# A gated linear recurrence stage: its convolution on TensorE, its root and scan one piece behind

## The chip, the cores and the metric

The kernel runs on one core of one Trainium2 chip. The metric is the device time of one execution in microseconds: 8486.05 us is the median of three runs before the change (8471.72 to 8500.62).

## The reference

One inference step of a decoder layer: projection, sparse attention, a recurrent branch, an output projection, a mixture of experts. The change touches the recurrent branch alone. It works on 512 channels for a prompt of 4096 positions and for 8 sequences of 4 new positions with stored states:

```python
def rglru_branch(xr, yg, conv_prev, h_prev, conv_w, conv_b, rg_wa, rg_ba, rg_wx, rg_bx, rg_lambda):
    n, t, _ = xr.shape
    xp = jnp.concatenate([conv_prev.astype(xr.dtype), xr], axis=1)
    xc = sum(conv_w[j] * xp[:, j:j + t] for j in range(CONV_WIDTH)) + conv_b
    conv_new = xp[:, t:]
    xb = xc.reshape(n, t, RG_BLOCKS, RG_BLOCK_W)
    r = jax.nn.sigmoid(jnp.einsum('ntkc,kcd->ntkd', xb, rg_wa).reshape(n, t, D_RNN) + rg_ba)
    i = jax.nn.sigmoid(jnp.einsum('ntkc,kcd->ntkd', xb, rg_wx).reshape(n, t, D_RNN) + rg_bx)
    log_a = -RG_C * r.astype(jnp.float32) * jax.nn.softplus(-rg_lambda.astype(jnp.float32))
    a = jnp.exp(log_a)
    b = jnp.sqrt(-jnp.expm1(2.0 * log_a)) * (i * xc).astype(jnp.float32)
    ...
    y = jnp.swapaxes(hs, 0, 1).astype(xr.dtype) * jax.nn.gelu(yg)
    return y, conv_new, h_last.astype(h_prev.dtype)
```

Between b and y stands the scan h = a*h + b along the positions. The outputs of the branch are y (to a scratch array in memory, read by the next stage), the last three convolution inputs and the last h, for the prompt and for each sampled sequence.

## The kernel before

The program is a row of stages (`build`), each closed by a barrier of all engines; inside a stage each engine runs a list of instructions written by hand, and waits on semaphores. The recurrent stage is `phase_recur`. Channels lie along the 128 partitions, so the 512 channels are four chunks c, and a chunk has three pieces k: positions 0 to 2047, 2048 to 4095, and the 32 sampled positions. The twelve pieces are `segs`; piece n is (n // 3, n % 3).

For each piece VectorE convolves (`convolve`: one product with bias, L1347, three multiply-adds, L1349), one piece ahead; TensorE multiplies the result by two block-diagonal gate matrices into PSUM (L1308, L1309); ScalarE makes two sigmoids (r and i, L1286, L1288), tanh (u), the tanh of the GELU, the exponential (a, L1295) and the square root (b, L1297); VectorE makes i*xc (L1360), a*a and the ratio (L1367, L1368), the GELU's product (L1372), the product with the root (L1374), the scan (L1377, with a copy of its last column, L1378) and the last product y (L1385). The 32 sampled positions are four steps of two small products (L1383, L1384) instead of a scan. GpSimd makes the inner polynomial of the GELU in three passes (L1270 to L1274).

SyncE issues all transfers in one order: the weights, `load(0)`, `load(1)`, then for each chunk the store of every piece's y to `rnnT` when its product is done (`y_done`), the prompt's states after piece k = 1, the sampled states after k = 2 (`rglru_sample` and three `conv_sample` stores, 4 bytes per element), and then a wait for these stores and `load(c + 2)`. A load is a chunk's xr and yg of 4096 positions, the 32 sampled columns, and three small loads of stored convolution states. The y, h and `hlast` buffers exist once, so the scan waits until the stores of the piece before have landed (`wait(e, s["stored"], stored_by(c, k))`):

```python
                    e.wait_ge(s["root"], n + 1)
                    ch.link(e.tensor_tensor(gi, gi, b[:, 0:l], ALU.mult))
                    wait(e, s["stored"], stored_by(c, k))
                    if k < 2:
                        ch.link(e.tensor_tensor_scan(h[:, 0:l], a[:, 0:l], gi, hlast[:, :] if k else 0.0, ALU.mult, ALU.add))
```

Of the kernel before, what the change touches and what calls it, by code (L numbers as in the profile page):

```python
# [20 lines left out]
P = 128  # L21
D = 1024
DC = D // P
SEQ = 4096
# [1159 lines left out]
def phase_recur(nc, A, S):  # L1184

    SEG = 2048
    with ExitStack() as ctx:
# [15 lines left out]
        names = "zeroed params chunk0 chunk1 conv gates r_done i_done a_done u_done ratio root inner tanh mult y_done stored act_own own pool_own consts softplus e1".split()  # L1203
# [3 lines left out]
        stored_by = lambda c, k: 16 * (9 * c + (0, 1, 4)[k])  # L1207
# [5 lines left out]
        with nc.Block() as block:  # L1213
            @block.sync
            def _(e):
# [22 lines left out]
                for c in range(RC):  # L1238
                    q = c % 2
                    at = slice(c * P, (c + 1) * P)  # L1240
                    for k in range(3):
                        e.wait_ge(s["y_done"], 3 * c + k + 1)
                        dst = slice(k * SEG, k * SEG + L(k))
                        e.dma_start(S["rnnT"][c, :, dst], y[:, 0:L(k)]).then_inc(s["stored"], 16)
                        if k == 1:
                            e.dma_start(S["rglru_prompt"][0:1, at].rearrange("o p -> p o"), hlast[:, :]).then_inc(s["stored"], 16)
                            e.dma_start(S["conv_prompt"][:, at].rearrange("j p -> p j"), x[:, q, SEQ:]).then_inc(s["stored"], 16)
                        if k == 2:
                            e.dma_start(S["rglru_sample"][:, at].rearrange("q p -> p q"),
                                        h[:, 0:SR].rearrange("p (q t) -> p q t", t=DECQ)[:, :, DECQ - 1]).then_inc(s["stored"], 16)  # L1250
                            for j in range(3):
                                e.dma_start(S["conv_sample"].rearrange("(q j) c -> q j c", j=3)[:, j, at].rearrange("q p -> p q"),
                                            xw[:, q, :, DECQ + j]).then_inc(s["stored"], 16)
# [3 lines left out]
                e.wait_ge(s["stored"], stored_by(RC, 0))  # L1257

            @block.gpsimd
            def _(e):  # L1260
# [3 lines left out]
                for n, (c, k) in enumerate(segs):  # L1264
                    src = yg[:, c % 2, k * SEG:(k + 1) * SEG] if k < 2 else ys[:, c % 2, :]
                    gg = gg2[:, n % 2, 0:L(k)]
                    loaded(e, c)
                    wait(e, s["y_done"], n - 1)
                    wait(e, s["pool_own"], 2 * n)
                    e.tensor_tensor(gg, src, src, ALU.mult).then_inc(s["pool_own"], 1)  # L1270
                    e.wait_ge(s["pool_own"], 2 * n + 1)
                    e.tensor_scalar(gg, gg, 0.044715, 1.0, ALU.mult, ALU.add).then_inc(s["pool_own"], 1)
                    e.wait_ge(s["pool_own"], 2 * n + 2)
                    e.tensor_tensor(gg, gg, src, ALU.mult).then_inc(s["inner"], 1)  # L1274

            @block.scalar
            def _(e):
                e.wait_ge(s["consts"], 1)
                e.activation(sp[:, 1, :], sp[:, 0, :], ACT.Exp, scale=-1.0).then_inc(s["e1"], 1)
                e.wait_ge(s["softplus"], 1)  # L1280
                for n, (c, k) in enumerate(segs):
                    l = L(k)
                    gi, gg = gi2[:, n % 2, 0:l], gg2[:, n % 2, 0:l]
                    e.wait_ge(s["gates"], n + 1)
                    wait(e, s["a_done"], n)
                    e.activation(r[:, 0:l], pa[:, 0:l], ACT.Sigmoid, bias=vec[:, 1, c:c + 1]).then_inc(s["r_done"], 1)  # L1286
                    wait(e, s["y_done"], n - 1)
                    e.activation(gi, px[:, 0:l], ACT.Sigmoid, bias=vec[:, 2, c:c + 1]).then_inc(s["i_done"], 1)  # L1288
# [1146 lines left out]
```

## Time and profile before

| what | value |
|---|---|
| median of three runs | 8486.05 us |
| the profiled execution: its own time | 8488.34 us |
| its span (first to last instruction) | 8486.2 us |
| busy in the span: TensorE, VectorE, ScalarE, GpSimd | 74%, 52%, 46%, 13% |
| the recurrent stage in it | from 5525 to 6032 us of the span |
| mean granted TensorE clock, share of full speed | 0.873 |

The busy shares are means over stages with different limits; the recurrent stage is some 6% of the span. Times in rows are microseconds from the start of the span. In the names, `rc_` tiles belong to the recurrent stage; PE is TensorE, DVE VectorE, ACT ScalarE, POOL GpSimd, SP SyncE; PEld is TensorE's load of weights. An f32 matmul leaves two MATMUL rows.

### The profile page before, as it was taken

What the parts mean: (1) busy time and instruction counts of PE and PEld (TensorE: products, weight loads), DVE (VectorE), ACT (ScalarE), POOL (GpSimd) and SP (SyncE); (2) the same over time, 40 slices, a digit from 0 to 9 for tenths busy, and PEclk for the clock granted to TensorE, in tenths of its full rate; (3) what the DMA queues carried; (4) which work ended last, traced back from release to release, by engine and by line L of the source; (5) the groups of instructions that cost most, each with busy time, mean ns of one, the idle gap of its engine ahead of it and who ended that gap; (6) DMA issues with size and microseconds to landing.
All of it is one profiled execution on the core that took longest, in us unless ns stands there. A gap on an engine that the chain in (4) does not pass through costs nothing. (4 is left out here: it accounts for less than half of the span.)

```text
span 8486.2 us, 113111 instructions
## 1 busy us (share of the span) xinstructions
PE 6263.9 (74%) x38431; PEld 4189.0 (49%) x38714; DVE 4448.6 (52%) x10781; ACT 3943.1 (46%) x7822; POOL 1095.8 (13%) x1571
## 2 busy tenths in 40 slices
PE   6999975887887788788888761711499929999950
PEld 2777752555555455555555541600255527667740
DVE  1122137888777878888888648256255511101126
ACT  0221225788877788888788730133233302212224
POOL 1222210000000000000000000022011143333334
PEclk8999987999999999999999975755688869999985
DMA  5221210000000000000000010234423238888877
GB/s 189 63 59 57 61 53 8 5 9 13 9 11 10 11 11 11 11 11 11 10 11 6 7 64 2 118 67 50 85 89 99 84 104 336 323 321 333 333 271 253
DMA packets 329210, 759.17 MB, mean 89 GB/s; under 512 B 123534, under 2 KB 187022, under 8 KB 285769
## 3 DMA queue, kind: packets, MB, share of 16 engines
q0 software_dynamic: 71520, 432.08, 13.8%
q1 hardware_dynamic: 257236, 321.70, 13.3%
q8 instruction: 222, 3.64, 0.2%
q14 instruction: 178, 1.45, 0.1%
q10 hardware_dynamic: 54, 0.30, 0.0%
HBM read 589.37 MB, written 162.62 MB: 89 GB/s over the span
## 5 line engine op out<-in xcount | busy, mean ns | idle before, releaser
L953 PE MATMUL at_pC<-at_mark,at_identb 128*128 128x256 bf16 (+1 forms) x5708 | 758.0, 283 | 382.8 <-DVE at_mark L1088 302.5
L1010 DVE CUSTOM_DVE_ANT_0 at_sm<-at_pS,at_drop 128x512 f32<-128x512 f32 (+3 forms) x1152 | 696.3, 642 | 319.3 <-PE at_pS L909 317.0
L953 PEld LDWEIGHTS at_pC<-at_mark,at_identb 128*128 128x128 bf16 x5708 | 531.9, 101 | 637.8 <-DVE at_mark L1088 462.6
L844 ACT ACTIVATE at_sm<-at_sm,at_negm 128x512 f32<-128x512 f32 (+3 forms) x1152 | 786.0, 696 | 58.8 <-DVE at_negm L1015 58.4
L909 PE MATMUL at_pS<-keep_KT,at_q 64*128 64x512 f32 (+3 forms) x2304 | 649.4, 642 | 205.0 <-DVE at_mx L1010 204.8
L1002 DVE SCALAR_TENSOR_TENSOR at_score<-at_relu,keep_IW,at_score 128x512 f32<-128x512 f32 (+3 forms) x994 | 660.5, 707 | 120.0 <-ACT at_relu L829 116.4
L930 PEld LDWEIGHTS at_pO<-at_pt_sb,keep_V 128*64 128x64 f32 x8448 | 471.7, 142 | 416.8 <-issue 290.5
L899 PE MATMUL at_pD<-keep_IKT,at_iq_stack 128*128 128x512 bf16 (+3 forms) x1989 | 521.1, 375 | 167.1 <-ACT at_relu L829 95.3
L829 ACT ACTIVATE at_relu<-at_pD 128x512 f32<-128x512 f32 (+3 forms) x1136 | 583.5, 569 | 104.6 <-PE at_pD L899 62.2
L919 PE MATMUL at_pT<-keep_ident,at_sm 128*128 128x128 f32 x4224 | 587.6, 281 | 40.9 <-DVE at_out L1024 32.5
L930 PE MATMUL at_pO<-at_pt_sb,keep_V 128*64 128x128 f32 x8448 | 614.5, 288 | 0.1
L2225 DVE TENSOR_TENSOR ex_gu<-ex_pg,ex_sg 128x256 f32<-128x256 f32 x98 | 41.6, 425 | 988.0 <-ACT ex_sg L2207 988.0
L919 PEld LDWEIGHTS at_pT<-keep_ident,at_sm 128*128 128x128 f32 x4224 | 474.0, 143 | 106.6 <-issue 96.2
L479 PE MATMUL pj_ptm<-keep_w_in,pj_hT 128*128 128x512 f32 (+1 forms) x1584 | 516.2, 488 | 0.0
L410 DVE TENSOR_TENSOR pj_ra<-pj_z,pj_rope 128x256 f32<-128x256 f32 x66 | 42.9, 651 | 858.0 <-ACT pj_z L384 858.0
L1791 POOL MEMSET sa_IQB<- 128x1024 f32 x1 | 1.0, 952 | 3773.3 <-POOLq L68 3773.3
L865 ACT ACTIVATE at_mark<-at_key_low,at_sigma 128x1536 bf16<-128x1536 uint16 (+15 forms) x390 | 451.6, 1165 | 73.8 <-DVEq L1084 73.1
L494 PE MATMUL pj_pcm<-pj_hT,keep_w_in 128*128 128x128 f32 x4224 | 477.1, 275 | 0.0
L494 PEld LDWEIGHTS pj_pcm<-pj_hT,keep_w_in 128*128 128x128 f32 x4224 | 474.3, 192 | 0.0
L835 ACT ACTIVATE at_pt_sb<-at_pT 128x512 f32<-128x512 f32 (+3 forms) x576 | 321.7, 559 | 302.5 <-PE at_pT L919 301.3
L2172 PE MATMUL ex_pg<-ex_wg,ex_xT 128*128 128x256 f32 x1568 | 379.5, 397 | 88.7 <-DMA ex_wu<-in_exp_w_up,ex_wi 83.0
L865 ACT ACTIVATE at_mark<-at_key_high,at_sigma 128x1280 bf16<-128x1280 int16 (+15 forms) x364 | 421.3, 1163 | 47.2 <-DVEq L1084 46.3
(418 smaller groups left out, 10910.2 us busy)
## 6 DMA issues: line engine op xcount, KB each, us to landing
scratch_ys<-ex_y SPq DMA_DIRECT2D x98, 512.0 KB, 2.7
ada_w_sb<-in_ada_w SPq DMA_DIRECT2D x12, 2048.0 KB, 8.1
scratch_x<-mx_x SPq DMA_DIRECT2D x33, 512.0 KB, 6.5
scratch_h<-mx_h SPq DMA_DIRECT2D x33, 512.0 KB, 2.7
cb_x<-scratch_x SPq DMA_DIRECT2D x33, 512.0 KB, 4.2
pj_x<-in_x_prompt SPq DMA_DIRECT2D x32, 512.0 KB, 3.5
mx_x<-in_x_prompt SPq DMA_DIRECT2D x32, 512.0 KB
out_y_prompt<-cb_out SPq DMA_DIRECT2D x32, 512.0 KB, 2.9
```

Source lines behind the costliest of these rows:

```text
L479: last = e.matmul(ptm[:, n, 0:b - a], hT[:, par, k, :], w[:, k, a:b], start=k == 0, stop=k == DC - 1)
L494: last = e.matmul(pcm[:, c // RC, c % RC, :], w[:, k, C_XR + c * P:C_XR + (c + 1) * P], hT[:, par, k, :], start=k == 0, stop=k == DC - 1)
L829: e.activation(r[:, n % 4, 0:b - a], pD[:, n % 2, 0:b - a], ACT.Relu).then_inc(s["relu"], 1)
L844: last = e.activation(row, row, ACT.Exp, bias=negm[:, x.group % 16, kv:kv + 1], scale=-1.0, accum_out=den[:, x.side, kv * G + x.g, x.c:x.c ...
L865: last = e.activation(mark[:, at], (lo if low else hi)[:, at], ACT.Sign, bias=trial, scale=-2.0 ** (v.what - (STRICT if low else HIGH)), a ...
L899: last = e.matmul(pD[:, n % 2, 0:b - a], IQH[:, side, k, h, :], keys[:, k, a:b], start=k == 0, stop=k == 1)
L909: last = e.matmul(pS[:, kv, 0:x.width], Q[rows, x.side, x.g, :], KT[rows, x.a:x.a + x.width], start=True, stop=True)
L919: last = e.transpose(pT[:, kv, j:j + P], sm[:, u % RING, kv, j:j + P], ident)
L930: last = e.matmul(pO[rows, x.g, :], V[:, (x.a + j) // P, rows], PTs[:, u % 2, kv, j:j + P], start=x.first and x.g == 0 and j == 0, stop=x. ...
L953: last = e.matmul(pC[:, side, 0:b - a], identb[:, :], mark[:, a:b], start=a == at.start, stop=not constant and b == at.stop)
L1002: e.scalar_tensor_tensor(at, r[:, n % 4, 0:b - a], w, at, ALU.mult, ALU.add).then_inc(s["acc"], 1)
L1010: last = e.tensor_tensor_reduce(sm[:, u % RING, kv, 0:x.width], pS[:, kv, 0:x.width], drop[:, o:o + x.width], -HD ** -0.5, -NEG, ALU.add, ...
```

## The change

The convolution moves from VectorE to TensorE: VectorE builds, once, sixteen 128 x 128 matrices with a tap's weights on the diagonal (`taps`), TensorE adds up four products per 512 columns in PSUM (`shift`), and ScalarE copies the sum out with its bias (`unload`). TensorE and the sigmoids now work in halves of 1024 columns, m = 0 to 19 (`halves`). ScalarE takes the GELU as one function, so GpSimd keeps only a small copy per chunk. The root of a piece stands behind the next piece's exponential (`root(n - 1)`), and on VectorE the product with the root, the scan and the last product stand behind the next piece's ratio (`recurrence(n - 1)`). y is written into the GELU's buffer, two deep; `hlast` and the sampled h have buffers per chunk; the stores have semaphores of their own (`written0/1`, `state0/1`), and no scan waits for them. The diff, cut to its core:

```diff
-    SEG = 2048
+    SEG, HALF = 2048, 1024
...
-        r = sb("rc_r", [P, SEG]); a = sb("rc_a", [P, SEG])
-        u = sb("rc_u", [P, SEG]); t1 = sb("rc_t1", [P, SEG]); t2 = sb("rc_t2", [P, SEG]); b = sb("rc_b", [P, SEG]); h = sb("rc_h", [P, SEG]); y = sb("rc_y", [P, SEG])
-        hlast = sb("rc_hlast", [P, 1])
-        pa = pb("rc_pa", [P, SEG]); px = pb("rc_px", [P, SEG])
+        a2 = sb("rc_a", [P, 2, SEG]); t2 = sb("rc_t", [P, 2, SEG])
+        r = sb("rc_r", [P, SEG]); u = sb("rc_u", [P, SEG]); b = sb("rc_b", [P, SEG]); h = sb("rc_h", [P, SEG])
+        taps = sb("rc_taps", [P, RC, 4, P])
+        hlast = sb("rc_hlast", [P, RC, 2]); hsm = sb("rc_h_sample", [P, RC, SR])
+        pc = pb("rc_pc", [P, 2, HALF]); pa = pb("rc_pa", [P, HALF]); px = pb("rc_px", [P, HALF])
...
+        halves = [(n, at) for n, (c, k) in enumerate(segs) for at in range(0, L(k), HALF)]
+        halves_by = lambda n: sum(m < n for m, _ in halves)
...
-                        e.dma_start(S["rnnT"][c, :, dst], y[:, 0:L(k)]).then_inc(s["stored"], 16)
+                        e.dma_start(S["rnnT"][c, :, dst], gg2[:, (3 * c + k) % 2, 0:L(k)]).then_inc(s[f"written{(3 * c + k) % 2}"], 16)
...
                     if c + 2 < RC:
-                        e.wait_ge(s["stored"], stored_by(c + 1, 0))
+                        e.wait_ge(s[f"state{q}"], 96 * (c // 2 + 1))
                         load(c + 2)
...
+                def unload(m):
+                    n, at = halves[m]
+                    c, k = segs[n]
+                    l = min(HALF, L(k) - at)
+                    e.wait_ge(s["shifted"], m + 1)
+                    wait(e, s["mult"], n - 1)
+                    e.activation(xc2[:, n % 2, at:at + l], pc[:, m % 2, 0:l], ACT.Identity, bias=vec[:, 0, c:c + 1]).then_inc(s["conv"], 1)
+
+                def sigmoids(m):
...
+                    e.wait_ge(s["gates"], m + 1)
+                    wait(e, s["a_done"], n)
+                    e.activation(r[:, at:at + l], pa[:, 0:l], ACT.Sigmoid, bias=vec[:, 1, c:c + 1]).then_inc(s["r_done"], 1)
+                    wait(e, s["y_done"], n - 1)
+                    e.activation(gi2[:, n % 2, at:at + l], px[:, 0:l], ACT.Sigmoid, bias=vec[:, 2, c:c + 1]).then_inc(s["i_done"], 1)
+
+                def root(n):
+                    l = L(segs[n][1])
+                    wait(e, s["y_done"], n)
+                    e.wait_ge(s["ratio"], n + 1)
+                    e.activation(b[:, 0:l], t2[:, n % 2, 0:l], ACT.Sqrt).then_inc(s["root"], 1)
+
+                unload(0)
                 for n, (c, k) in enumerate(segs):
...
+                    for m in range(halves_by(n), halves_by(n + 1)):
+                        if m + 1 < len(halves):
+                            unload(m + 1)
+                        sigmoids(m)
...
+                    wait(e, s[f"written{n % 2}"], 16 * (n // 2))
+                    e.activation(gg2[:, n % 2, 0:l], gate, ACT.Gelu_apprx_tanh).then_inc(s["gelu"], 1)
+                    e.activation(a2[:, n % 2, 0:l], r[:, 0:l], ACT.Exp, scale=c8[:, 1, c:c + 1]).then_inc(s["a_done"], 1)
+                    if n:
+                        root(n - 1)
+                root(len(segs) - 1)
...
+                def shift(m):
+                    n, at = halves[m]
+                    c, k = segs[n]
+                    q = c % 2
+                    loaded(e, c)
+                    if k == 2:
+                        e.wait_ge(s["window"], c + 1)
+                    wait(e, s["conv"], m - 1)
...
+                def gates(m):
+                    n, at = halves[m]
+                    c, k = segs[n]
+                    e.wait_ge(s["conv"], m + 1)
+                    wait(e, s["i_done"], m)
+                    wait(e, s["r_done"], m)
...
+                shift(0)
+                for m in range(len(halves)):
+                    if m + 1 < len(halves):
+                        shift(m + 1)
+                    gates(m)
...
+                for n in range(len(segs)):
+                    ratio(n)
+                    if n:
+                        recurrence(n - 1)
+                recurrence(len(segs) - 1)
```

Three places of the order in which instructions stand. The first is ScalarE in the first chunk, from the sigmoids of the second piece to the root; before:

```order
L1286 ACT_TABLE_LOAD
L1286 ACTIVATE rc_r<-rc_pa,rc_vec 128x2048
L1288 ACTIVATE rc_i<-rc_px,rc_vec 128x2048
L1291 ACTIVATE rc_u<-rc_r,rc_c 128x2048
L1293 ACTIVATE rc_g<-rc_g 128x2048
L1295 ACT_TABLE_LOAD
L1295 ACTIVATE rc_a<-rc_r,rc_c 128x2048
L1297 ACT_TABLE_LOAD
L1297 ACTIVATE rc_b<-rc_t 128x2048
```

And after the change, where L1284 is the copy of a half's convolution and L1300 the root of the piece before:

```order
L1284 ACTIVATE rc_xc<-rc_pc,rc_vec 128x32
L1292 ACTIVATE rc_r<-rc_pa,rc_vec 128x1024
L1294 ACTIVATE rc_i<-rc_px,rc_vec 128x1024
L1311 ACTIVATE rc_u<-rc_r,rc_c 128x2048
L1314 ACT_TABLE_LOAD
L1314 ACTIVATE rc_g<-rc_yg 128x2048
L1315 ACT_TABLE_LOAD
L1315 ACTIVATE rc_a<-rc_r,rc_c 128x2048
L1300 ACT_TABLE_LOAD
L1300 ACTIVATE rc_b<-rc_t 128x2048
L1284 ACTIVATE rc_xc<-rc_pc,rc_vec 128x1024
```

A load of the GELU's table has come in between tanh and the exponential, the root now reads the ratio of the piece before, and the next copy stands behind it. In the whole stage there are 47 table loads where there were 36.

The second place is TensorE at the change from chunk 1 to chunk 2 after the change; L1334 are the tap products, L1346 and L1347 the gates:

```order
L1346 MATMUL rc_pa<-rc_xc,rc_wa 128x512
L1347 MATMUL rc_px<-rc_xc,rc_wx 128x512
L1334 MATMUL rc_pc<-rc_x,rc_taps 128x512 x8
L1346 MATMUL rc_pa<-rc_xc,rc_wa 128x32
L1347 MATMUL rc_px<-rc_xc,rc_wx 128x32
L1334 MATMUL rc_pc<-rc_x,rc_taps 128x512 x8
```

The eight tap products of the new chunk's first half, which read the loaded x, stand ahead of the gates of the old chunk's small piece (128x32). Before, the same place held gates alone:

```order
L1308 MATMUL rc_pa<-rc_xc,rc_wa 128x512
L1309 MATMUL rc_px<-rc_xc,rc_wx 128x512
L1308 MATMUL rc_pa<-rc_xc,rc_wa 128x32
L1309 MATMUL rc_px<-rc_xc,rc_wx 128x32
L1308 MATMUL rc_pa<-rc_xc,rc_wa 128x512
L1309 MATMUL rc_px<-rc_xc,rc_wx 128x512
```

The third place is VectorE after the change, from the second piece's ratio to the first piece's last product:

```order
L1391 TENSOR_TENSOR rc_i<-rc_i,rc_xc 128x2048
L1395 TENSOR_TENSOR rc_t<-rc_a 128x2048
L1396 SCALAR_TENSOR_TENSOR rc_t<-rc_t,rc_u 128x2048
L1404 TENSOR_TENSOR rc_i<-rc_i,rc_b 128x2048
L1407 SCALAR_TENSOR_TENSOR rc_h<-rc_a,rc_i 128x2048
L1408 COPY rc_hlast<-rc_h 128x1
L1416 TENSOR_TENSOR rc_g<-rc_h,rc_g 128x2048
```

The first three rows belong to the second piece, the last four to the first (L1407 is its scan); the four passes of the convolution and the GELU's product are gone from this list.

## Rows read from the trace of the kernel before

**Rows 1.** The page's first line.

```profile
span 8486.2 us, 113111 instructions
```

**Rows 2.** Stretches: length, busy time (instructions) of PE, PEld, DVE, ACT, POOL, granted clock, DMA share, GB/s.

```profile
5561.47:5665.43 103.96, 23.20 (x40) 10.13 (x41) 86.32 (x47) 37.03 (x28) 44.36 (x13) 0.58 0.16 59
5665.43:5766.66 101.23, 20.37 (x39) 8.72 (x38) 65.60 (x43) 35.74 (x27) 25.46 (x9) 0.59 0.47 63
5766.66:5868.90 102.24, 18.09 (x35) 8.01 (x34) 65.87 (x38) 35.74 (x27) 25.53 (x9) 0.58 0.49 62
5868.90:5971.67 102.77, 17.78 (x34) 7.43 (x32) 49.46 (x45) 34.45 (x26) 12.77 (x6) 0.58 0.37 21
5971.67:6032.06 60.39, 0.00 (x0) 0.00 (x0) 0.00 (x1) 0.00 (x0) 0.00 (x0) 0.50 0.60 1
```

**Rows 3.** Waits in the stage: who for whom, total us, times, longest.

```profile
DVE rc_h L1377 <- DMA out_conv_sample<-rc_xw: 72.8, 3, 25.5
...
DVE rc_h L1383 <- DMA out_conv_prompt<-rc_x: 18.2, 4, 16.2
```

**Rows 4.** VectorE's groups in the stage: shapes, count, busy us, mean ns, idle before.

```profile
L1349 DVE SCALAR_TENSOR_TENSOR rc_xc<-rc_x,rc_cw,rc_xc 128x2048 f32<-128x2048 f32 x24 | 85.4, 3556 | 0.9
...
L1347 DVE TENSOR_SCALAR rc_xc<-rc_x,rc_cw,rc_vec 128x2048 f32<-128x2048 f32 x8 | 20.6, 2571 | 8.2 <-DMA rc_xw<-in_state_conv 8.0
...
L1384 DVE TENSOR_TENSOR rc_h<-rc_h,rc_i 128x8 f32<-128x8 f32 x16 | 2.8, 175 | 0.5
```

**Rows 5.** ScalarE in order of time: start, us, instruction, then idle time before.

```profile
5625.19 1.28 ACT L1295 ACT_TABLE_LOAD   x1
5626.48 2.00 ACT L1295 ACTIVATE rc_a<-rc_r,rc_c 128x2048 f32<-128x2048 f32 x1
...
5636.39 0.29 ACT L1286 ACTIVATE rc_r<-rc_pa,rc_vec 128x32 f32<-128x32 f32 x1
```

**Rows 6.** The same view in the stage before: a function over 1056 columns.

```profile
5471.27 1.08 ACT L1825 ACTIVATE sa_lgt<-sa_lgt 128x1056 f32<-128x1056 f32 x1 [7.68 <-DVE sa_lgt L1968]
```

**Rows 7.** VectorE in order of time: a large piece's recurrence.

```profile
5635.37 2.29 DVE L1374 TENSOR_TENSOR rc_i<-rc_i,rc_b 128x2048 f32<-128x2048 f32 x1
5637.70 4.49 DVE L1377 TENSOR_TENSOR_SCAN rc_h<-rc_a,rc_hlast,rc_i 128x2048 f32<-128x2048 f32 x1
...
5642.40 2.29 DVE L1385 SCALAR_TENSOR_TENSOR rc_y<-rc_h,rc_t 128x2048 f32<-128x2048 f32 x1
```

**Rows 8.** TensorE in order of time: one burst of gate products, two rows (x2) each.

```profile
5582.35 2.05 PE L1308 MATMUL rc_pa<-rc_xc,rc_wa 128*128 128x512 f32 x2 [67.36 <-DVE rc_xc L1349]
5584.19 1.92 PE L1309 MATMUL rc_px<-rc_xc,rc_wx 128*128 128x512 f32 x2
5585.89 1.91 PE L1308 MATMUL rc_pa<-rc_xc,rc_wa 128*128 128x512 f32 x2
...
5588.88 1.02 PE L1308 MATMUL rc_pa<-rc_xc,rc_wa 128*128 128x512 f32 x2
5589.74 1.02 PE L1309 MATMUL rc_px<-rc_xc,rc_wx 128*128 128x512 f32 x2
```

**Rows 9.** SyncE's queue: its waits for stores ahead of a load: total us, times, longest.

```profile
SPq L1230 <- DMA out_conv_sample<-rc_xw: 103.2, 2, 52.7
```

**Rows 10.** In order of time: the first load's issue, VectorE's first use, chunk 2's load.

```profile
5543.93 0.58 SPq L1230 DMA_DIRECT2D rc_x<-scratch_xrT  x1
...
5561.47 4.73 DVE L1347 TENSOR_SCALAR rc_xc<-rc_x,rc_cw,rc_vec 128x2048 f32<-128x2048 f32 x1 [7.97 <-DMA rc_xw<-in_state_conv]
...
5718.39 0.35 SPq L1230 DMA_DIRECT2D rc_x<-scratch_xrT  x1
```

**Rows 11.** Tile view of out_conv_sample: its twelve stores, issue to landing.

```profile
DMA to landing us min/median/max: 32.1/44.1/54.4
```

**Rows 12.** Issues in the stage: count, KB each, median us from issue to landing.

```profile
scratch_rnnT<-rc_y SPq DMA_DIRECT2D x8, 1024.0 KB, 5.7
...
out_rglru_sample<-rc_h SPq DMA_DIRECT2D x4, 4.0 KB, 19.9
```

More of the change, by code:

```diff
@@ L1263, in _ @@
                 e.memset(x[:, :, 0:3], 0.0).then_inc(s["zeroed"], 1)
-                for n, (c, k) in enumerate(segs):
-                    src = yg[:, c % 2, k * SEG:(k + 1) * SEG] if k < 2 else ys[:, c % 2, :]
-                    gg = gg2[:, n % 2, 0:L(k)]
+                for c in range(RC):
                     loaded(e, c)
[L1268 to L1274, printed above, removed]
+                    e.tensor_copy(xw[:, c % 2, :, 3:], xs[:, c % 2, :].rearrange("p (q t) -> p q t", t=DECQ)).then_inc(s["window"], 1)
             @block.scalar
@@ L1296, in _ @@
-                    e.wait_ge(s["ratio"], n + 1)
-                    e.activation(b[:, 0:l], t1[:, 0:l], ACT.Sqrt).then_inc(s["root"], 1)
+                    gate = yg[:, c % 2, k * SEG:(k + 1) * SEG] if k < 2 else ys[:, c % 2, :]
+                    wait(e, s[f"written{n % 2}"], 16 * (n // 2))
+                    e.activation(gg2[:, n % 2, 0:l], gate, ACT.Gelu_apprx_tanh).then_inc(s["gelu"], 1)
+                    e.activation(a2[:, n % 2, 0:l], r[:, 0:l], ACT.Exp, scale=c8[:, 1, c:c + 1]).then_inc(s["a_done"], 1)
@@ new lines, in gates @@
+                def gates(m):
+                    n, at = halves[m]
+                    c, k = segs[n]
+                    e.wait_ge(s["conv"], m + 1)
+                    wait(e, s["i_done"], m)
+                    wait(e, s["r_done"], m)
+                    for a in range(0, min(HALF, L(k) - at), CUT):
+                        l = min(CUT, L(k) - at - a)
+                        xc = xc2[:, n % 2, at + a:at + a + l]
+                        e.matmul(pa[:, a:a + l], wa[:, c, :], xc, start=True, stop=True)
+                        last = e.matmul(px[:, a:a + l], wx[:, c, :], xc, start=True, stop=True)
+                    last.then_inc(s["gates"], 1)
@@ L1315, in _ @@
                 e.wait_ge(s["params"], 16 * 28)
+                for c in range(RC):
+                    for j in range(4):
+                        last = e.tensor_scalar(taps[:, c, j, :], S["ident"][:, :], cw[:, c, j:j + 1], None, ALU.mult)
+                last.then_inc(s["taps"], 1)
                 ch.link(e.tensor_scalar(sp[:, 2, :], vec[:, 3, :], -1.0, None, ALU.mult))
@@ L1364, in _ @@
+                    e.wait_ge(s["i_done"], halves_by(n + 1))
+                    e.wait_ge(s["conv"], halves_by(n + 1))
+                    e.tensor_tensor(gi2[:, n % 2, 0:l], gi2[:, n % 2, 0:l], xc2[:, n % 2, 0:l], ALU.mult).then_inc(s["mult"], 1)
                     e.wait_ge(s["a_done"], n + 1)
                     e.wait_ge(s["u_done"], n + 1)
-                    wait(e, s["root"], n)
-                    ch.link(e.tensor_tensor(t1[:, 0:l], a[:, 0:l], a[:, 0:l], ALU.mult))
-                    e.scalar_tensor_tensor(t1[:, 0:l], t1[:, 0:l], 1.0, u[:, 0:l], ALU.add, ALU.mult).then_inc(s["ratio"], 1)
@@ L1370, in _, with recurrence @@
-                    src = yg[:, c % 2, k * SEG:(k + 1) * SEG] if k < 2 else ys[:, c % 2, :]
-                    e.wait_ge(s["tanh"], n + 1)
-                    ch.link(e.scalar_tensor_tensor(t2[:, 0:l], gg2[:, n % 2, 0:l], 1.0, src, ALU.add, ALU.mult))
+                    wait(e, s["root"], n - 1)
+                    ch.link(e.tensor_tensor(t, a, a, ALU.mult))
+                    e.scalar_tensor_tensor(t, t, 1.0, u[:, 0:l], ALU.add, ALU.mult).then_inc(s["ratio"], 1)
+                def recurrence(n):
+                    c, k = segs[n]
+                    l = L(k)
+                    a, gi, gg = a2[:, n % 2, 0:l], gi2[:, n % 2, 0:l], gg2[:, n % 2, 0:l]
+                    e.wait_ge(s["mult"], n + 1)
```

88 lines of the change are left out of this document (28 added, 60 removed).

## The prediction

> **What bounds the kernel now.** The page's first line gives the span, 8486.2 us [rows 1]; the profiled execution took 8488.34 us, 2.3 us over the median of the runs. The change touches one stage alone, so I read the view of stretches, cut where the first load lands and where the last product of each chunk ends [rows 2]. The four chunks take 104.0, 101.2, 102.2 and 102.8 us, and after the last product 60.4 us pass in which nothing computes until the next stage starts. In a chunk VectorE is busy for 49 to 86 us, ScalarE for some 36, TensorE for some 20: VectorE sets the pace, with gaps. The view of waits says what the gaps are [rows 3]: three times, 72.8 us together, a scan waits until the 4-byte stores of the chunk before have landed, and 18.2 us more go to the small store of the prompt's convolution state. The groups show the largest single piece of VectorE's work: the convolution costs 85.4 + 20.6 = 106.0 us in the eight large pieces [rows 4].
>
> I number the pieces 0 to 11 (pieces 2, 5, 8 and 11 are the small ones, of 32 columns) and write y0 to y11 for the end of a piece's last product. Before, y2, y5, y8 and y11 are 5665.4, 5766.7, 5868.9 and 5971.7 [rows 2]. All that follows y11 is the same 60.4 us, so the whole forecast is one number: where y11 comes to stand.
>
> **The change, part by part.** *Prices.* A ScalarE function over 2048 columns takes 2.0 us, a table load 1.28, so that the function starts 1.3 later, and a function over 32 columns 0.3 [rows 5]. For 1024 columns I take 1.1, by a row of 1056 columns [rows 6]. On VectorE the product with the root, the scan (4.49), its copy and the last product take 2.3 + 4.5 + 0.2 + 2.3 = 9.3 us for a large piece [rows 7]; for a small one eight steps of 0.175 and two small products, some 2.1 with their links [rows 4]. An f32 matmul of 512 columns is two rows: in a burst's first 6 us one starts 1.70 us after the other (the engine at 1.2 GHz), later 0.86 (2.4 GHz) [rows 8]. Eight tap matmuls, one half piece, are thus 6.9 to 13.6 us, four gate matmuls 3.4 to 6.8. I take the fast end plus 2.6 for the first 6 us after a long idle, since the burst shown became fast after some 6 us, and 4.7 for gates behind a short idle; the ends go into the range.
>
> *Engine sums.* VectorE loses the convolution and the GELU's product, and keeps five passes of 2.3 and a scan, 16.2 us per large piece. TensorE has 24 matmuls where there were 8: 20.6 us. ScalarE has six half functions, four whole ones and four table loads, 6.6 + 8.0 + 5.2 = 19.8 us. GpSimd's three GELU passes go. If these ran side by side a piece would cost 20.6 us against more than 25 before; they do not.
>
> *A loop through three engines.* ScalarE's second sigmoid of piece n waits for y(n-2), whose buffer it reuses. The root of piece n-1 now stands behind the exponential of piece n, and y(n-1) needs that root. So from one product to the next everything is in a row: sigmoid 1.1, the second half's gates 4.7, two sigmoids 2.1, tanh 2.0, load 1.3, GELU 1.9, load 1.3, exponential 2.0, load 1.3, root 1.9, VectorE 9.3: 28.9. VectorE's ratio of piece n ends 1.5 us after that root and stands ahead of the recurrence, and handovers cost some 0.7: about 31 us for a large piece.
>
> *First chunk.* The load lands at 5561.5 as before [rows 10]. The 16 products that make the tap matrices fit the 7.97 us in which VectorE waits there [rows 10]; if they took longer, each us would be added once. TensorE does three shifts and two gate groups, 32 matmuls, 27.5 + 2.6: 5591.6. Sigmoids to exponential of piece 0, 10.6: 5602. Copy, load and sigmoids of piece 1's first half 4.5, gates 5.3, sigmoids 2.1, tanh to exponential 8.5, load and root 3.2, VectorE's ratio 1.5, then 9.3: y0 is 5637. Piece 2's GELU waits until the store of piece 0 has landed, 5.7 [rows 12]; its rest and the root of piece 1 take 5.0, VectorE 9.3: y1 is 5657. Then 1.1 + 4.7 + 2.1 + 8.5, the ratio of piece 3 (4.6), the small recurrence 2.1 and handovers: y2 is 5681, 15.6 us later than now.
>
> *Chunk changes.* SyncE's order stays: store y2, the 4-byte stores, wait for them, load the next chunk. From y2 to the load's issue 53.0 us pass [rows 2, 10], 51.6 of it the wait itself in the mean of the two [rows 9], and the load lands 17.5 us after its issue [rows 10]. Now VectorE has no scan that waits for these stores; instead the wait moves to the load. TensorE's shift of the next chunk's first half stands ahead of the small piece's gates, and ScalarE's copy ahead of its sigmoids (both shown by the order above). So pieces 5 and 4 cannot end before the load: 53.0 + 17.5 + shift 9.5 + copy, small functions, four loads and root 4 9.6 + VectorE 9.3 + handovers 1.1 = 100: y4 is 5781. What covers this is piece 3 and the sums of piece 4 alone, some 31 us after y2; ScalarE then stands idle for about 60 us where VectorE stood for some 24. Another 23 as for y2, with the gates faster: y5 is 5804, and a chunk takes 123 us against 101.2. The second change is the same: y8 is 5927.
>
> *The last chunk.* No load follows, so no such wait. But SyncE sends the store of piece 9 (y9 is 5927 + 31 = 5958) behind four 4-byte stores issued at y8. Three of these land 32.1, 44.1 and 54.4 us after their issue, each some 11 behind the one before, where one ahead of them takes 19.9 [rows 11, 12]: landings come in the order of issue. I therefore let store 9 land with them, at 5981, not 5.7 us after its issue. GELU 11 waits for it, and root 10 stands behind GELU 11: 5.0 + 9.3, then the small piece's root and recurrence and handovers 3.7: y11 is 5999.
>
> The sum: 5999 - 5971.7 = 27.3 us later. 8488.3 + 27.3 - 2.3 = **8513 us**. A measurement here tells 0.3% (25.5 us) from no change, so this lies just past that line.
>
> *Where pages of the Trainium skill speak to this.* On the table loads, "ScalarE: Activation LUTs", section "What ACT_TABLE_LOAD costs", puts every switch of set at 2.66 us, drain included, and tells authors to batch by set; the change makes 47 loads of 36. In this trace a function starts 1.3 us after its load began, so the trace decides and the page's price is not used. By it the 11 added loads would cost 29 us where 1.3 gives 14, and the time would be some 15 us longer. On the order of landings, "DMA: Bandwidth & Descriptors", section "Queues, rings and completion order", says a transfer's semaphore write lands only after every earlier write of that DMA engine. That is what I let store 9 do; no row of before has a large store behind 4-byte ones.
>
> **The rivals.**
> *Large stores overtake the small ones.* Store 9 then lands at 5964, GELU 11 is no longer held by it, and y11 is about 5981, 9 us later: 8496 us. Against it stand the landings in order [rows 11]; for it, that no row shows a large store in this place.
> *Faster: the 4-byte stores land sooner.* Both chunk changes and the 60.4 us at the end hang on that landing, so each us of it counts three times. It decides from 9 us on: at 44 instead of 53 the stage is as long as now. If all landed like the first one, in 19.9 [rows 12], 3 x 33 us would go: 8414 us. For it: the stores now read small buffers of their own. Against it: number, size and target of the stores are unchanged, and both waits of before agree [rows 9].
> *TensorE stays at 1.2 GHz.* Its gaps in the loop (up to 11 us while VectorE scans) may keep it slow, as the granted clock of 0.58 to 0.59 in the chunks shows for now [rows 2]. Then a large piece is 24 x 1.70 = 41 us, first of all on TensorE: some 10 us more than the loop for each of eight pieces and a few for each shift behind a load, about 85 to 110 in all: 8600 to 8625 us. Against it: 16 to 24 matmuls per piece in long runs, and the burst of before became fast after some 6 us [rows 8].
>
> **How the numbers follow.** Forecast 0.62, overtaking 0.17, sooner landings 0.07, slow clock 0.06, the rest (a cover or a wait I misjudged, to either side) 0.08. The forecast's own range is 8500 to 8530: gates and shifts at the fast end take 7 us off, at the slow end they add 2.1 per loop. The range for 8 in 10 takes in overtaking and, above, slow gates in most loops: 8490 to 8540. Slower by over 0.3% is somewhat more than half of the forecast (27 against a line of 25.5, and its upper side is wider) plus the slow clock: 0.53. Within 0.3%: the rest of the forecast, and overtaking: 0.38. Faster: 0.09.
>
> **What would show it.** Right: in the changed profile TensorE's first shift of a new chunk ends an idle time of some 60 us, released by the load, twice; the stretches y2 to y5 and y5 to y8 are about 123 us; the convolution is gone from VectorE, which is busy for some 37 us of a chunk; ScalarE waits for a store's landing ahead of the last GELU, and a large piece that nothing holds takes about 31 us from product to product. Wrong: chunks under 105 us, a load that is issued less than 44 us after its chunk's last product, a product-to-product time near 21 us, or a granted clock of half speed through the stage.

## The result, and the profile after

| | before | changed |
|---|---|---|
| median of 5 runs | 8483.35 us (8470.90 to 8500.62) | 8445.29 us (8420.11 to 8446.83) |
| ratio, 95% interval | | 0.9948 (0.9935 to 0.9961) |
| profiled execution | 8488.34 us | 8446.37 us |
| stage: issue of its first load to the next stage's first load | 488.1 us | 424.0 us |

The changed kernel is 0.5% faster; the forecast was 0.3% slower. The stage is 64 us shorter, but all that follows it took 2477.7 us in this execution against 2454.1. That remainder spread from 2449 to 2480 us over the runs below and differed by 12 us between two executions of one and the same kernel, so from here on I compare lengths of the stage, each from one profile. They too spread: the kernel before with both placing edits below took 411.4 us in one execution and 393.4 in another, so differences well under 18 us tell little.

The page's first line [rows 1]:

```profile
span 8444.6 us, 113983 instructions
```

The view of stretches, cut as before at the small pieces' last products, y2, y5, y8 and y11 (the first begins near the landing of the first load) [rows 2]:

```profile
5561.00:5677.67 116.67, 88.65 (x203) 39.37 (x202) 41.18 (x30) 65.80 (x55) 0.21 (x1) 0.89 0.13 48
5677.67:5777.47 99.80, 49.85 (x108) 21.99 (x108) 34.30 (x27) 45.28 (x39) 0.22 (x1) 0.74 0.38 64
5777.47:5876.10 98.63, 46.74 (x108) 20.86 (x108) 34.31 (x27) 45.27 (x39) 0.21 (x1) 0.76 0.42 65
5876.10:5928.10 52.00, 6.08 (x12) 2.66 (x12) 27.49 (x24) 23.58 (x22) 0.00 (x0) 0.57 0.47 33
5928.10:5966.90 38.80, 0.00 (x0) 0.00 (x0) 0.03 (x1) 0.00 (x0) 0.00 (x0) 0.50 0.36 11
```

VectorE's busy time (third column) fell from 66 to 34 us a chunk, and the two middle chunks are hardly shorter: no engine is busy for more than half of them. What is much shorter is the last chunk, 52.0 us in place of 102.8, and the stretch at the end, where nothing computes: 38.8 us in place of 60.4.

The waits in the stage:

```profile
PE rc_pc L1334 <- DMA rc_xw<-in_state_conv: 127.7, 3, 45.8
...
ACT rc_xc L1284 <- PE rc_pc L1334: 102.9, 5, 37.2
...
ACT rc_g L1314 <- DMA scratch_rnnT<-rc_g: 4.7, 2, 2.6
...
SPq L1232 <- DMA out_conv_sample<-rc_xw: 58.3, 2, 29.8
```

No scan waits for a store any more [rows 3]. TensorE waits for the load, ScalarE for TensorE, and SyncE for the stores ahead of the load, as forecast; but SyncE's two waits are 58.3 us together, not 103.2 [rows 9]. The cause is the landing of the state stores, that is the time from a store's issue until its semaphore tells that it is done. The tile view of out_conv_sample gives the shortest, the median and the longest, against 32.1/44.1/54.4 [rows 11]; the issues give the median of the large stores and of rglru_sample, against 5.7 and 19.9 [rows 12]:

```profile
DMA to landing us min/median/max: 15.6/22.7/31.7
```

```profile
scratch_rnnT<-rc_g SPq DMA_DIRECT2D x8, 1024.0 KB, 5.9
...
out_rglru_sample<-rc_h_sample SPq DMA_DIRECT2D x4, 4.0 KB, 14.4
```

The 4-byte state stores land in half to three quarters of the time. The large stores take as long as before, and number and size of the packets are the same. SyncE's issues in order of time show it once: store of y2, the state stores, then the load of chunk 2, now 31.2 us behind the store of y2 [rows 10]:

```profile
5677.67 0.33 SPq L1246 DMA_DIRECT2D scratch_rnnT<-rc_g  x1
5678.05 0.43 SPq L1251 DMA_DIRECT2D out_rglru_sample<-rc_h_sample  x1
5678.52 1.83 SPq L1254 DMA_DIRECT2D out_conv_sample<-rc_xw  x3
5708.90 0.35 SPq L1232 DMA_DIRECT2D rc_x<-scratch_xrT  x1
```

### The profile page after: what moved, and what is told of

It is laid out like the page before. It is cut to its first block and busy times, and to the rows that moved or that the text cites. A ratio compares the mean times of both kernels' runs of the same rounds, so it can differ in the third digit from the quotient of the medians.

```text
span 8444.6 us, 113983 instructions
## 1 busy us (share of the span) xinstructions
PE 6401.7 (76%) x39002; PEld 4242.0 (50%) x39002; DVE 4319.9 (51%) x10733; ACT 3981.5 (47%) x7869; POOL 994.8 (12%) x1539
## 5 line engine op out<-in xcount | busy, mean ns | idle before, releaser
L844 ACT ACTIVATE at_sm<-at_sm,at_negm 128x512 f32<-128x512 f32 (+3 forms) x1152 | 786.3, 697 | 58.7 <-DVE at_negm L1015 58.3
L899 PE MATMUL at_pD<-keep_IKT,at_iq_stack 128*128 128x512 bf16 (+3 forms) x2272 | 585.2, 378 | 141.9 <-ACT at_relu L829 89.6
L919 PE MATMUL at_pT<-keep_ident,at_sm 128*128 128x128 f32 x4224 | 588.6, 282 | 40.9 <-DVE at_out L1024 32.5
```

The source lines that it names most:

```text
L844: last = e.activation(row, row, ACT.Exp, bias=negm[:, x.group % 16, kv:kv + 1], scale=-1.0, accum_out=den[:, x.side, kv * G + x.g, x.c:x.c ...
L899: last = e.matmul(pD[:, n % 2, 0:b - a], IQH[:, side, k, h, :], keys[:, k, a:b], start=k == 0, stop=k == 1)
L919: last = e.transpose(pT[:, kv, j:j + P], sm[:, u % RING, kv, j:j + P], ident)
```

## The experiments

Six theories are told apart. **A, S, W:** the small source tile, the separate counts, or GpSimd's silence (or the GELU function) make the 4-byte stores land sooner. **G:** where the program or its outputs lie in memory does. **L:** the order one piece behind costs time. **T:** the landing can be taken off the path by issuing those stores earlier. "Landings" are those of rglru_sample (median), and of the three conv_sample stores as min/median/max. The runs were made on several chips, on which the kernel before took 8478 to 8503 us in the median; each ratio is against the kernel before on the same chip. The diffs are cut to their core (`...`).

**The two kernels once more**, unchanged.

> The kernel before, unchanged, profiled a second time. In the first profile the 4-byte stores at a chunk's end land 19.9 us (rglru_sample) and 32.1/44.1/54.4 us (three conv_sample stores) after their issue; in the changed kernel 14.4 and 15.6/22.7/31.7. Theory A (the change's own buffers, above all the small tile that the sampled state is stored from, make the stores land sooner): here again about 20 and 32 to 54, and from the last product to the next stage about 60 us. Theory B (how fast such stores land belongs to the run or to where the outputs lie in memory, not to an edit): here some other value, such as 14 and 16 to 32, with the last product to the next stage near 39 us; each us of it counts about twice to three times in the time.

> The changed kernel, unchanged, profiled a second time. Theory A: again about 14 and 16 to 32 us from issue to landing, 30 us from a chunk's last product to the next load's issue, 39 us at the end. Theory B: another value than in its first profile, and the same as in the other kernels of this chip.

Before: 8482.27 us, landings 20.3 and 30.8/42.8/53.6, stage 482.7. Changed: 8442.12 us, 14.8 and 16.6/24.9/33.3, stage 428.1. The landing belongs to the kernel, not to the run.

**A small source tile alone.**

```diff
+hsm = sb("rc_h_sample", [P, RC, SR])
...
-    h[:, 0:SR].rearrange(...)[:, :, DECQ - 1]).then_inc(s["stored"], 16)
+    hsm[:, c, :].rearrange(...)[:, :, DECQ - 1]).then_inc(s["stored"], 16)
```

> The kernel before with one part of the change: the sampled steps write h into a small tile of their own (128 x 4 x 32), which rglru_sample is stored from; all else as before. Theory A: rglru_sample lands in about 14 us instead of 20 and the conv_sample stores in 16 to 32, so the stage ends some 40 to 60 us sooner. Theory B: the same landings as the unchanged kernel on this chip, and the same time within 10 us.

8500.24 us, landings 19.1 and 29.9/42.8/54.2: as before. A falls, and with it the reason that the prediction gave for its rival of sooner landings.

**Own buffers and separate counts alone**, in the kernel before.

```diff
-dma_start(S["rnnT"][c, :, dst], y[:, 0:L(k)]).then_inc(s["stored"], 16)
+dma_start(S["rnnT"][c, :, dst], y[:, n % 2, 0:L(k)]).then_inc(s[f"written{n % 2}"], 16)
...
-e.wait_ge(s["stored"], stored_by(c + 1, 0))
+e.wait_ge(s[f"state{q}"], 96 * (c // 2 + 1))
...
-wait(e, s["stored"], stored_by(c, k))
```

> The kernel before with one part of the change alone: the stored states in buffers of their own, two y buffers and the four counts in place of the one, so that the scan no longer waits for the stores of the chunk before (convolution on VectorE, tanh GELU and the order of the functions stay). Theory S (the one shared count, or the waits on it, makes the landing of the 4-byte stores long): landings fall to about 14 us for rglru_sample and 16, 24, 32 us for conv_sample, the load of chunk 2 is issued 31 us behind the small piece's product, and the time is 8350 to 8385. Theory G (landing is a property of the program as a whole, its memory or its code's place, and not of these waits): landings stay at 20 and 32, 43, 54 us, the wait of 73 us leaves VectorE's scan and the load is issued 53 us behind the product as before; chunks 1 and 3 are then bound by VectorE's own some 68 us (two large pieces of some 27 us and a small one), chunk 2 by its load, and the time is 8380 to 8430. If the wait only moves (rival M, as the prediction had it), chunks stay near 100 us and the time is within 20 us of the kernel before.

8417.95 us, ratio 0.9910 (0.9890 to 0.9931). Tile view of out_conv_sample:

```profile
DMA to landing us min/median/max: 32.2/42.9/55.1
```

S falls: the landing is as long as before, and the load is issued 53.5 us behind the store of y2 (5658.2 to 5711.7). The time falls all the same, to chunks of 89, 88 and 63 us, since the pieces of the other chunk now run during that wait. In this order of the functions the wait moved to the load and was mostly covered.

**A longer program**: 160 memsets of one column on GpSimd, where it waits for the load.

```diff
+for i in range(160):
+    e.memset(junk[:, i:i + 1], 0.0)
```

> The kernel before with 160 memsets of one column each on GpSimd at the start of the recurrent stage, while GpSimd would wait for the load: they change the length of the program and nothing that the stage waits for. Theory G (the place of code or buffers in memory sets the landing of the 4-byte stores): the landings may move from 20 and 32, 43, 54 us by several us, in either direction. Theory S (waits and counts set it): landings within 2 us of those of the kernel before, time within 20 us of it.

8488.96 us, landings 20.0 and 31.0/42.7/54.1: unmoved. Only the prompt's two small stores moved, conv_prompt's from 18.0 us to 10.7.

**GELU as one function alone.**

```diff
-e.tensor_tensor(gg, src, src, ALU.mult)
...
-e.activation(gg, gg, ACT.Tanh, scale=math.sqrt(2 / math.pi)).then_inc(s["tanh"], 1)
+e.activation(gg, gate, ACT.Gelu_apprx_tanh).then_inc(s["tanh"], 1)
...
-ch.link(e.scalar_tensor_tensor(t2, gg2, 1.0, src, ALU.add, ALU.mult))
```

> The kernel before with one part of the change alone: GELU as one function of ScalarE, so that GpSimd computes nothing in the stage and VectorE's product of tanh and gate falls away. Theory W (what GpSimd does in the stage, or the table of the GELU function in the program, sets how fast the 4-byte stores land): landings near 14 us for rglru_sample and 16 to 33 us for conv_sample, time 8400 to 8430. Theory G (where the program or its buffers lie in memory) and theory C (the convolution on TensorE): landings stay at 20 and 32, 43, 54 us; VectorE gives back 2.3 us per large piece at most outside the wait, and the time is within 20 us of the kernel before.

8407.95 us, stage 387.2. Tile view of out_conv_sample:

```profile
DMA to landing us min/median/max: 16.8/24.3/31.2
```

This part alone brings the short landing, as W had it; the convolution on TensorE (theory C of the expectation) is not needed for it.

**The outputs elsewhere**: no instruction changes, only the order in which the outputs are declared, or 4 MB of scratch ahead of the other scratch, or both.

```diff
-for name, shape, _ in _OUT:
+for name, shape, _ in reversed(_OUT):
...
-_SCRATCH = [("mod", ...
+_SCRATCH = [("pad", [1024, 1024], F32), ("mod", ...
```

> The kernel before with its outputs declared in the opposite order and one more scratch tensor of 4 MB declared ahead of the others; nothing else. Theory G (the place in memory of the stores' destination sets their landing): landings move from 20 and 32, 43, 54 us by over 5 us, and the time with them, about three us for each us. Theories W and C: landings within 2 us of those of the kernel before.

> The kernel before with outputs declared in the opposite order and 4 MB more scratch, as before_placed, now with an interval. Theory G (the place in memory of the destination sets the landing): landings again near 14.5 us for rglru_sample and 16, 26, 34 for conv_sample, 8395 to 8425, below the changed kernel's 8442. Rival (the single run of before_placed was a chance): 8470 to 8510 with landings of 32, 43, 54.

> The kernel before with its outputs declared in the opposite order alone. Theory G by the order of the outputs: landing near 16, 26, 34 us and 8395 to 8425. If the scratch does it: landings of 32, 43, 54 us and 8470 to 8510.

> The kernel before with 4 MB of scratch declared ahead of the others alone. Theory G by the scratch, which moves what is placed behind it: landings near 16, 26, 34 us and 8395 to 8425. If the order of the outputs does it: landings of 32, 43, 54 us and 8470 to 8510.

Both edits: 8409.18 us in the single run; again, 8392.05 us, ratio 0.9912 (0.9891 to 0.9933). Scratch alone: 8469.42, stage 466.0, landings 18.3 and 28.3/39.0/48.7, about a tenth shorter than before and far from the short ones. The order of the outputs alone: 8394.82, stage 391.2; its tile view of out_conv_sample:

```profile
DMA to landing us min/median/max: 15.9/22.8/30.3
```

So the short landing needs neither the GELU nor any other instruction: it comes with the order of the outputs in the kernel before as it is, and takes 71 to 97 us off its stage. Stretches of the repeated run, cut where the small pieces' y stores are issued, against [rows 2]:

```profile
5557.00:5660.17 103.17, 22.80 (x40) 9.87 (x41) 85.93 (x47) 37.02 (x28) 43.96 (x12) 0.58 0.16 58
5660.17:5741.93 81.76, 20.49 (x38) 8.87 (x37) 65.59 (x43) 35.74 (x27) 25.52 (x9) 0.58 0.42 78
5741.93:5821.10 79.17, 20.61 (x38) 8.87 (x37) 65.69 (x43) 35.74 (x27) 25.52 (x9) 0.59 0.46 81
5821.10:5898.90 77.80, 17.37 (x34) 7.41 (x32) 48.55 (x39) 34.46 (x26) 12.75 (x6) 0.61 0.31 28
5898.90:5933.42 34.52, 0.00 (x0) 0.00 (x0) 0.00 (x0) 0.00 (x0) 0.00 (x0) 0.50 0.52 1
```

VectorE and ScalarE are as busy as in [rows 2], to within an us; the three later chunks are 19 to 25 us shorter each and the end 26. VectorE's waits for conv_sample's landing, in the same run:

```profile
DVE rc_h L1377 <- DMA out_conv_sample<-rc_xw: 4.2, 2, 3.5
```

It was 72.8 [rows 3].

**The changed kernel with its outputs elsewhere**: both edits, and rglru_sample and conv_sample declared first.

```diff
-for name, shape, _ in _OUT:
+for name, shape, _ in _OUT[-2:] + _OUT[:-2]:
```

> The changed kernel with the same two edits. Theory G: landings move from 14 and 16, 24, 33 us by over 5 us. Theories W and C: landings within 2 us of those of the changed kernel, time within 20 us of it.

> The changed kernel with rglru_sample's and conv_sample's outputs declared ahead of the other outputs; nothing else. Theory G: it may fall into either placement. If the landings are 32, 43, 54 us, the load is issued 53 us behind the small piece's product and the time is near my forecast, 8495 to 8530; if they are 16, 24, 33 us, the time stays within 15 us of the changed kernel's 8445 and the try decides nothing.

8441.21 us, landings 15.8 and 16.8/25.2/37.1; 8443.91 us, 16.1 and 16.1/25.2/37.7. Both stay near the short landing, so the changed kernel with the long one was not seen.

**Root and recurrence at once** in the changed kernel.

```diff
-if n:
-    root(n - 1)
+root(n)
...
-    if n:
-        recurrence(n - 1)
+    recurrence(n)
```

> The changed kernel with one part undone: the root stands right behind its own piece's exponential and the recurrence right behind its own ratio, not one piece behind. Theory L (the loop: sigmoid of piece n, gates, sigmoids, tanh, GELU, exponential, root of n-1, recurrence of n-1, sigmoid of n+1, 31 us a large piece, is what a large piece costs): undone, the sigmoid waits for a product two pieces back, a large piece costs ScalarE's 19.8 us plus some 3 to 5 of waiting for the ratio, about 24 to 28 us, and the first product comes at 5617 instead of 5634; the whole is 50 to 75 us faster than the changed kernel, 8370 to 8395 us. The rival (a piece behind is needed to keep ScalarE from waiting for VectorE's ratio, as the change is meant): ScalarE waits 4.6 us for each ratio, and the stage is 20 to 40 us slower than the changed kernel.

8371.77 us, ratio 0.9847 (0.9831 to 0.9864). Its first three chunks, cut in the same way:

```profile
5562.00:5648.48 86.48, 68.68 (x159) 30.79 (x158) 34.40 (x27) 48.47 (x42) 0.21 (x1) 0.89 0.16 58
5648.48:5716.04 67.56, 42.80 (x98) 18.97 (x97) 34.41 (x27) 45.04 (x40) 0.80 (x1) 0.80 0.49 95
5716.04:5790.97 74.93, 46.54 (x108) 20.84 (x107) 34.48 (x27) 45.16 (x40) 0.21 (x1) 0.80 0.46 85
```

L holds: the same instructions take 30 us less in the first chunk, 32 and 24 in the next two. The order one piece behind costs some 70 us of time.

**State stores earlier**: conv_prompt's and conv_sample's stores at the chunk's start, in the changed kernel and in the variant with the root at once; in that variant also behind the first y store of the chunk (only the place differs).

```diff
+e.wait_ge(s["window"], c + 1)
+e.dma_start(S["conv_prompt"]...).then_inc(s[f"early{q}"], 16)
+for j in range(3):
+    e.dma_start(S["conv_sample"]..., xw[:, q, :, DECQ + j]).then_inc(s[f"early{q}"], 16)
...
-e.wait_ge(s[f"state{q}"], 96 * (c // 2 + 1))
+e.wait_ge(s[f"early{q}"], 64 * (c // 2 + 1))
```

> The changed kernel with the conv_prompt and conv_sample stores issued at the start of each chunk, behind the window copy, where their data are already there, and with the load of chunk c+2 waiting for these alone. Theory T (the landing of these stores is on the path at both chunk changes and at the end of the stage): the load of chunk 2 is issued within 3 us of the small piece's product in place of 31, ScalarE's idle times of 36 and 37 us at the chunk changes shrink to 10 to 15, the tail of 39 us falls to 20, and the time falls by 50 to 75 us to 8370 to 8395. Rival (the many small packets take the engines from the large stores, or the loop of the pieces takes the place of the wait): less than 20 us gained.

> The variant with root and recurrence of the same piece at once, and the early stores as well. Theory T and L together: 8310 to 8345, some 30 to 60 us under the variant with root at once alone (8372). Rival (with a shorter loop VectorE is the bound, and the wait at chunk changes was already hidden by it): within 15 us of 8372.

> Root and recurrence of the same piece at once, and the conv_prompt and conv_sample stores issued right behind the y store of the chunk's first piece in place of the chunk's start. Theory Q (in the variant with the stores at the chunk's start the gain was given back because the y store of the first piece, which a GELU waits for, and the issues of the load queue behind the 4-byte packets): ScalarE's waits for y stores of 25 us in all go to under 5, chunk changes stay free of the landing, and the time is 8310 to 8340. Rival (the packets of load and stores take the same engines wherever they are issued): 8350 to 8370, as with the stores at the chunk's start.

In the changed kernel nothing is gained: 8445.87 us, ratio 0.9942 (0.9922 to 0.9963), stage 434.2. The load is issued within 1 us of the store of y2 and the end is 20 us, as T had it, but T's 50 to 75 us did not come: the y store now queues behind the 4-byte stores, and a GELU waits for it. ScalarE's wait and the tile view of rc_g:

```profile
ACT rc_g L1316 <- DMA scratch_rnnT<-rc_g: 62.3, 4, 28.0
```

```profile
DMA to landing us min/median/max: 1.4/8.4/41.7
```

With the root at once: 8360.11 us, ratio 0.9856 (0.9829 to 0.9884), stage 350.8; behind the first y store 8370.15 us, 0.9854 (0.9836 to 0.9873), stage 349.4, where 360.3 and a ratio of 0.9847 were. No gain is shown: the ratios are no lower, and 10 us of stage are less than two executions of one kernel differed by. ScalarE still waits for y stores, 25.4 us in the one place and 16.6 in the other, where under 5 were expected of the second.

**Own buffers and one GELU**, convolution on VectorE, order as before, outputs and scratch placed as in the run with both edits; then also the stores of conv_prompt and conv_sample behind the first y store, conv_sample's out of rc_xs.

> The kernel before with two parts of the change, own buffers for the stored states and GELU as one function, its convolution still on VectorE and its order as it was, and the outputs and scratch placed as in before_placed. Theory (at the fast landing the tap matrices and the order one piece behind are what costs): chunks of 62 to 70 us bound by VectorE, the next stage starts near 5880, and the time is 8320 to 8375, below both kernels. Rival (the load's 31 us wait and its 17.5 us landing are not covered by the other chunk's pieces): chunks near 80 us, 8380 to 8410.

> As own_buffers_gelu_placed, with the conv_prompt and conv_sample stores issued behind the y store of the chunk's first piece (conv_sample's from rc_xs, which holds the same numbers) and the load of chunk c+2 waiting for these alone. Theory (the tail behind the last product, 41 us there, is their landing; chunk changes are already covered): the tail falls to 20 to 25 us, chunks stay at 70 us, and the time is 8325 to 8340, 15 to 25 us under that variant. Rival (as with the early stores before: y stores and loads queue behind the small packets and give it back): within 10 us of it.

8352.22 us, ratio 0.9855 (0.9839 to 0.9872), stage 348.5; with early stores 8355.42, 0.9838 (0.9821 to 0.9855), stage 346.4. Stretches of the first:

```profile
5637.43:5708.50 71.07, 20.18 (x37) 8.64 (x36) 52.36 (x40) 39.91 (x30) 0.00 (x0) 0.62 0.54 90
5708.50:5780.03 71.53, 20.65 (x37) 8.89 (x36) 52.36 (x40) 39.92 (x30) 0.00 (x0) 0.60 0.54 89
5780.03:5844.20 64.17, 18.07 (x34) 7.71 (x32) 44.04 (x36) 38.63 (x29) 0.00 (x0) 0.61 0.43 34
5844.20:5885.96 41.76, 0.00 (x0) 0.00 (x0) 0.00 (x0) 0.00 (x0) 0.00 (x0) 0.50 0.55 1
```

Without tap matrices this is level with the root at once and beats both kernels. Early stores again brought no gain, where 15 to 25 us were expected: the end is 39.7 us, since rglru_sample's store then lands 23.7 to 34.3 us after its issue, behind the others.

## Why the prediction was wrong

**The step that failed** is the landing of the state stores: "From y2 to the load's issue 53.0 us pass" and "All that follows y11 is the same 60.4 us". Both were carried over from before. Measured: 31.2 and 32.5 us, and 38.8. The prediction had this as a rival, at a chance of 0.07, "each us of it counts three times": 3 x 22 = 66 us off 8513 gives 8447, and 8446.37 was measured. Its reasons did not decide it: small buffers of their own did not shorten the landing, and the same number, size and target of the stores did not keep it. (That it fits so closely has luck in it: the last chunk counted the landing a fourth time, and the 23.6 us more behind the stage took that back.) Two of the prediction's own signs of being wrong came true, chunks under 105 us (99.8 and 98.6) and a load issued less than 44 us after its chunk's last product; both follow from a landing that is 22 us shorter.

| us | forecast | measured |
|---|---|---|
| y0, y1, y2 | 5637, 5657, 5681 | 5634.2, 5653.2, 5677.6 |
| y2 to y4, y2 to y5 | 100, 123 | 76.1, 99.8 |
| y8 to y9 (a large piece that nothing holds) | 31 | 31.1 |
| y8 to y11 | 72 | 52.0 |
| y11 to the next stage | 60.4 | 38.8 |

**What was right.** The loop through three engines is 31.1 us, and its undoing gave 70 us. The first chunk is late by 12 us where 16 were forecast. The wait moved from VectorE's scan to the load; ScalarE's idle time there is 37 us, short of the forecast 60 by little more than the landing. That the loss would have shown at the old landing is an estimate: both the kernel before (stage 391 to 411 us with the short landing, three runs; 483 and 488 with the long one) and the forecast (515 with the long one, 424 to 436 measured with the short one, four runs) differ by nearly the same, some 80 to 90 us, as four terms of some 21 do.

**The change itself, at equal landing, is a loss of the size forecast**: mean stages 429 against 399 us, and ratios of 0.9948 (0.9935 to 0.9961) against 0.9912 (0.9891 to 0.9933), 0.36% or some 31 us, and single runs on one chip, both kernels with both placing edits, 8441.21 against 8409.18; the forecast was 27. It lies where the forecast put it. Stretch by stretch, against the repeated run of the kernel before at the short landing, the first chunk is 13.5 us longer (forecast 15.6), the next two 18.0 and 19.5 (22 and 21), the last 25.8 shorter (31), and the end 4.3 longer (0). What made the changed kernel faster than the kernel before is the landing, and of the change's parts the one-function GELU is the one with which it came.

**Table loads.** The GELU's load starts at 5688.67 and its function at 5689.96:

```profile
5688.67 1.28 ACT L1314 ACT_TABLE_LOAD   x1
5689.96 1.91 ACT L1314 ACTIVATE rc_g<-rc_yg 128x2048 f32<-128x2048 f32 x1
```

It is 1.29 us, as for the other sets; the 2.66 us of the Trainium skill, "ScalarE: Activation LUTs", section "What ACT_TABLE_LOAD costs", were not seen here either. The rule to batch calls by set, which the prediction names beside it, stands on that page of the Trainium skill in the section "Table sets: the hidden batching unit".

**One reading of before.** The prediction has y8 at 5868.9; the small product of that chunk ends at 5870.1, so the last two chunks took 103.4 and 101.6 us. No term of the sum goes by it.

**The other rivals.** Overtaking falls: in the changed kernel with earlier state stores, y stores issued behind them landed up to 41.7 us after their issue, where 5.9 is the median without. The Trainium skill, "DMA: Bandwidth & Descriptors", section "Queues, rings and completion order", has a transfer's semaphore write wait for that engine's earlier writes, and the trace of that run agrees. In the changed kernel itself it hardly came to bear: GELU 11 waited 2.1 us, where the forecast had y11 lose 18 to that wait (5999 against 5981), since the last state store ahead landed 1 us after the issue of y9's store. The slow clock falls too: 0.74 to 0.89 of full speed were granted in the three chunks that hold nearly all of TensorE's work (0.57 in the last, with 6 us of products).

**Open.** That the place of the outputs in memory decides is argued: the traces hold no addresses, and shown is only that the order of declaration does it with no instruction changed. Why the GELU function brings the short landing in the old order is not shown either; 4 MB of scratch shortened it by a tenth only, and 160 instructions not at all. A program of another size may place the outputs differently. The changed kernel with the long landing was tried for twice and not met, so the 8495 to 8530 us expected of it stay untested.

## What to carry to other kernels

A duration taken over from the kernel before is a property of that whole program: where one transfer's landing stands three or four times on the path, price what the forecast becomes if it moves, and give that case its weight. Before a gain is put down to an edit, run the old kernel with its outputs declared in another order. And an instruction moved one piece behind on one engine can close a loop through three: add up the row from one product to the next, not each engine's sum.

## What the runs showed of the hardware

1024 packets of 4 bytes landed, with no small store ahead of them, in 14 to 16 us in some programs and in 18 to 20 in others (medians). The last of three more such stores behind them took 30 to 38 us at the longest in the first kind and 49 to 55 in the second. The kernel before showed both, with the same instructions, by the order of its outputs alone. Three programs were profiled twice, and both profiles had the same kind. Large stores (5.7 and 5.9 us) did not share it. conv_prompt's store, of 384 such packets, had two levels of its own, 16.6 to 18.4 and 10.0 to 10.7 us (medians), and did not change with the others: in the padded kernel it was short while theirs was long.

Much of the landing is not the moving of packets. The stretch between the last packet of the four state stores and the next load's issue, first in the kernel before, then in the changed one (the last two numbers are DMA share and GB/s):

```profile
5689.00:5718.39 29.39, 6.84 (x14) 2.58 (x12) 6.61 (x3) 11.99 (x7) 0.00 (x0) 0.67 0.00 0
5693.00:5708.90 15.90, 0.00 (x0) 0.00 (x0) 13.54 (x6) 5.37 (x4) 0.00 (x0) 0.50 0.00 0
```

For 29.4 of 53.1 us and for 15.9 of 31.2 us the profile has no packet on any of the core's DMA engines, while SyncE waits for the landing: 13.5 of the 22 us of difference lie there. Why it lasts that long the traces do not show.
